# Conditioning units taken in pairs and fours, a column quadrant of TensorE per quarter of the columns, turned by VectorE block transposes

## The reference, cut to what matters

```python
def _modulate(x, g, shift, scale):
    return _rms(x, g) * (1 + scale[:, None, :]) + shift[:, None, :]
...
for l in range(DEPTH):                      # DEPTH = 2
    mod = jax.nn.silu(c) @ p['ada_w'][l] + p['ada_b'][l]      # (1024) @ (1024, 6144)
    sh1, sc1, g1, sh2, sc2, g2 = jnp.split(mod, 6, axis=-1)
    xm = _modulate(x, p['norm_g'][l, 0], sh1, sc1)
...
    x = x + g1[:, None, :] * y
    xm = _modulate(x, p['norm_g'][l, 1], sh2, sc2)
    x = x + g2[:, None, :] * _swiglu(xm, ...)
```

## Time and profile before

| what | value |
|---|---|
| median of 3 runs | 1632.27 us (1632.23 to 1632.67) |
| the profiled execution | 1630.69 us |
| its span in the trace | 1628.4 us |
| PE busy | 1553.3 us, 95% of the span |
| DVE, ACT, POOL busy | 703.1, 375.5, 746.8 us |
| chain that ended last | PE 87%, DVE 5%, ACT 3%, issue 2%, DMA 1% |

### The profile page before, as it was taken

How to read it: one execution, slowest core, us unless ns; L and a number is a source line. 1 busy time by engine, 2 the same in 40 slices (tenths; PEclk the granted TensorE clock), 3 DMA queues, 4 the chain that set the end, 5 groups by cost and what they waited for, 6 DMA issues and landing times.

```text
span 1628.4 us, 30979 instructions
## 1 busy us (share of the span) xinstructions
PE 1553.3 (95%) x11910; PEld 1454.5 (89%) x11910; DVE 703.1 (43%) x1280; ACT 375.5 (23%) x877; POOL 746.8 (46%) x424
## 2 busy tenths in 40 slices
PE   4999999999999999999999996888999999999999
PEld 2898898999999999999988795656899999999998
DVE  4502354443333123346864056787454442144421
ACT  3411555221110011111220122676321110011100
POOL 3244432444445544455544443144355555455553
PEclk9999999999999999999999998899999999999999
DMA  9245323334444333443222153121122222222231
GB/s 362 81 164 176 113 88 100 128 131 145 141 151 148 131 117 132 151 169 121 93 76 73 70 206 107 54 78 31 52 78 77 83 95 81 72 83 77 85 115 65
DMA packets 53906, 183.18 MB, mean 112 GB/s; under 512 B 6232, under 2 KB 8672, under 8 KB 53584
## 3 DMA queue, kind: packets, MB, share of 16 engines
q1 hardware_dynamic: 51136, 174.63, 31.6%
q10 hardware_dynamic: 2704, 7.64, 1.2%
HBM read 171.69 MB, written 10.55 MB: 112 GB/s over the span
## 4 chain that ended last, share of the span: by engine, by line
PE 87%; DVE 5%; ACT 3%; issue 2%; DMA 1%; POOL 0%; ACTq 0%; DVEq 0%; SPq 0%; POOLq 0%
PE psum L542 67%; PE psum L590 7%; PE psum L552 3%; PE psum L930 1%; DVE act_lo L1430 1%; PE psum L973 1%; PE psum L833 1%; PE psum L917 1%; DVE tmp L1419 1%; DMA raw<-in_w_stream 1%; PE psum L563 1%; PE psum L945 1%; PE psum L853 1%; PE psum L730 1%; ACT sc L1289 1%
## 5 line engine op out<-in xcount | busy, mean ns | idle before, releaser
L473 POOL TENSOR_SCALAR w_hi<-raw 128x1024 fp32r<-128x1024 f32 (+1 forms) x184 | 212.1, 1153 | 748.2 <-PE psum L542 628.8
L475 POOL TENSOR_TENSOR w_lo<-raw,w_hi 128x1024 fp32r<-128x1024 f32 (+1 forms) x184 | 485.1, 2636 | 15.3
L542 PE MATMUL psum<-act_hi,w_hi 128*128 128x288 f32 x2144 | 473.3, 302 | 11.3 <-POOL w_lo L475 4.8
L542 PE MATMUL psum<-act_lo,w_hi 128*128 128x288 f32 x2144 | 463.0, 297 | 0.0
L542 PE MATMUL psum<-act_hi,w_lo 128*128 128x288 f32 x2144 | 462.8, 297 | 0.0
L542 PEld LDWEIGHTS psum<-act_hi,w_hi 128*128 128x128 f32 x2144 | 345.8, 190 | 30.7 <-issue 17.5
L542 PEld LDWEIGHTS psum<-act_hi,w_lo 128*128 128x128 f32 x2144 | 348.0, 190 | 0.0
L542 PEld LDWEIGHTS psum<-act_lo,w_hi 128*128 128x128 f32 x2144 | 347.1, 189 | 0.0
L542 PE MATMUL psum<-hid_hi,w_hi 128*128 128x288 f32 x704 | 151.1, 296 | 0.0
L542 PE MATMUL psum<-hid_lo,w_hi 128*128 128x288 f32 x704 | 150.8, 296 | 0.0
L542 PE MATMUL psum<-hid_hi,w_lo 128*128 128x288 f32 x704 | 150.8, 296 | 0.0
(11 more groups left out here) (259 smaller groups left out, 1684.9 us busy)
## 6 DMA issues: line engine op xcount, KB each, us to landing
raw<-in_w_stream SPq DMA_DIRECT2D x153, 512.0 KB, 3.3
ada_ring<-in_ada_w SPq DMA_DIRECT2D x80, 512.0 KB, 3.3
raw<-in_w_down SPq DMA_DIRECT2D x32, 704.0 KB, 4.0
ada_first<-in_ada_w SPq DMA_DIRECT2D x8, 1024.0 KB, 12.5
line_rep<-line SPq DMA_DIRECT2D x8, 352.0 KB, 4.5
line<-line_rep SPq DMA_DIRECT2D x8, 352.0 KB, 5.2
x<-in_x SPq DMA_DIRECT2D x4, 576.0 KB, 5.7
dec<-line SPq DMA_DIRECT2D x8, 288.0 KB, 4.0
```

The lines of the kernel that those rows point to most:

```text
L473: pool.tensor_scalar(hi, src, 1.0, 0.0, ALU.mult, ALU.add).then_inc(hi_split, 1)
L475: pool.tensor_tensor(lo, src, hi.bitcast(F32), ALU.subtract).then_inc(lo_split, 1)
L542: last = mm(psum[:, b + half, 0:n_cols], weights[wp][:, k, :], parts[ap][:, k, half * HT:half * HT + n_cols], start=(k == 0 and n == 0), s ...
```

## The change

- `matvec` now takes two or four units at once. Quadrant j computes the columns 32j to 32j+31 of each of them over all eight k tiles: 32 matmuls, each with 32 stationary columns and 64 (a pair) or 128 (a four) moving columns. The result stands in PSUM as two full rows per quadrant, so that nothing is left to add.
- ACT's row copies and PE's turns are gone. DVE turns the rows by a block transpose of 32x32 (`ve.transpose`) and adds the bias.
- Units 16 to 47 go in 16 pairs, behind every second projected unit; a pair fills both slots of the ring, and its loads wait for the pair before. Units 48 to 95 go in 12 fours, ten of them behind four projected units of the first FFN and two around its first down units; each has a buffer of 2 MB (`ada_quad`) in the place of the unused second activation buffer, whose four loads wait for the four before. None is left among the queries of the attention.
- The loops of PE that held one conditioning unit behind each projected unit are written out or hold four units.
- At the start the table for the line of biases goes first, the squares of the input have three buffers and not one, the first four pairs of conditioning units are computed ahead of the first step, and the others stand between the steps.

```diff
 
-                if n0 >= ADA_START + 2:
-                    sp.wait_ge(ada_mv, i * 2 + (n0 - ADA_START - 1))
+                p = (n0 - ADA_START) // 2
+                if p >= 1:
+                    sp.wait_ge(ada_mv, i + p)
                 sp.dma_start(ada_ring[:, n0 % 2].rearrange("p k c -> p (k c)"), ada_w[i * 2 + n0]).then_inc(ada_in[n0 % 2], 16)
+
+            def load_quad(q, parts):
+
+                if q == 0:
+                    sp.wait_ge(unit_done, U_OUT + 8)
+                else:
+                    sp.wait_ge(quad_mv, q)
+                for j in parts:
+                    sp.dma_start(ada_quad[:, j].rearrange("p k c -> p (k c)"), ada_w[ADA_QUADS + 4 * q + j]).then_inc(quad_in, 16)
 
...
             sp.dma_start(sml[:, :], small).then_inc(params_ready, 16)
-            sp.dma_start(oh_sb[:, :], oh_line).then_inc(line_in, 16)
-            sp.dma_start(tab_sb[:, :], table).then_inc(line_in, 16)
             for g in range(KT):
+                if g == 6:
+                    sp.wait_ge(line_done, 2)
+                    sp.dma_start(line_dram[:, 0, :], line_sb[:, :]).then_inc(line_stored, 16)
                 if g >= 6:
-                    sp.wait_ge(ada_row_mm, g - 5)
+                    sp.wait_ge(first_mv, g - 5)
                 sp.dma_start(ada_first[:, g % 6].rearrange("p u k c -> p u (k c)"),
                              ada_w[g:g + KT + 1:KT].rearrange("u p n -> p u n")).then_inc(ada_first_in[g], 16)
                 if g < 2:
                     load_unit(g)
...
                 load_rows(h)
-            load_pairs(U_O, 19, 30)
+            load_pairs(U_O, 9, 30)
+
+            def load_four(u0, q):
+
+                for j in range(4):
+                    load_unit(u0 + j)
+                    if j >= 1:
+                        load_quad(q, (j - 1,) if j < 3 else (2, 3))
+
+            for n in range((FH - 1) // 2):
+                load_four(U_FFN0 + 2 + 4 * n, n)
             sp.wait_ge(state_stored, 128)
 
...
 
-            def matvec(out, w, done):
-
-                for kk in range(2):
+            def matvec(rows, w, done):
+
+                for k in range(KT):
                     for j in range(4):
-                        last = mm(out(slice(32 * j, 32 * j + 32)), cs_col(2 * j + kk), w(2 * j + kk), start=(kk == 0), stop=(kk == 1))
+                        r = slice(32 * j, 32 * j + 32)
+                        last = mm(by_unit(rows[r]), cs_col(k), w(k)[:, :, r], start=(k == 0), stop=(k == KT - 1))
                 last.then_inc(done, 1)
 
-            def ada_rows(n0, i=0):
-                s = n0 % 2
-                pe.wait_ge(ada_in[s], i * 16 + 16 * ((n0 - ADA_START) // 2 + 1))
-                matvec(lambda r: psum[r, row_bank(n0), 0:P], lambda k: ada_ring[:, s, k, :], ada_mv)
-
-            def ada_turn(n0, i=0):
-
-                pe.wait_ge(row_ready, i * 2 + (n0 - ADA_START + 1))
-                mm(psum[:, 5, bass.ds(i * 4 + 2 * n0, 2)], row_sb[:, n0 % 2, :], ada_sel, start=True, stop=True).then_inc(ada_done, 1)
-
-            def modulate(n0, i=0, first=False):
-                if not first:
-                    ada_turn(n0 - 1, i)
-                ada_rows(n0, i)
+            def modulate(p):
+
+                for half in range(2):
+                    pe.wait_ge(ada_in[half], 16 * (p + 1))
+                matvec(pair_rows(p), lambda k: ada_ring[:, :, k, :], ada_mv)
+
+            def modulate_four(q, i=0):
+
+                pe.wait_ge(quad_in, i * 64 + 64 * (q + 1))
+                pe.wait_ge(quad_free, i + (q + 1))
+                matvec(quad_rows, lambda k: ada_quad[:, :, k, :], quad_mv)
 
             def project_values(u0, a, tails, ada0=None, between=None):
...
-            pe.wait_ge(params_ready, 64)
-            norm_sums(N_IN)
             pe.wait_ge(line_in, 32)
...
@@ -621,35 +641,29 @@
                 for u in range(2):
                     project(u, 0, act[0], ready=(lo_ready[A_IN], 1), k0=k, k1=k + 1 if k < KT - 1 else None)
 
-            pe.wait_ge(sel_ready, 1)
+            def first_pair(g):
+
+                pe.wait_ge(ada_first_in[g], 16)
+                if g >= 4:
+                    pe.wait_ge(mod_first, g - 3)
+                elif g == 2:
+                    pe.wait_ge(ms_read, 1)
+                matvec(first_rows(g), lambda k: ada_first[:, g % 6, :, k, :], first_mv)
+
+            pe.wait_ge(silu_ready, 3)
+            for g in range(4):
+                first_pair(g)
             for g in range(KT):
-                pe.wait_ge(ada_first_in[g], 16)
-                if g >= 2:
-                    pe.wait_ge(ada_row_ready, g - 1)
-                elif g == 1:
-                    pe.wait_ge(ms_read, 1)
-                matvec(lambda r: psum[r, 4 + 3 * (g % 2), 0:2 * P].rearrange("p (u c) -> p u c", u=2),
-                       lambda k: ada_first[:, g % 6, :, k, :], ada_row_mm)
-                if g >= 2:
-                    first_step(g - 2)
-                pe.wait_ge(ada_row_ready, g + 1)
-                if g >= 1:
-                    pe.wait_ge(mod_first, g)
-                for u in range(2):
-                    mm(psum[:, 5, 2 * (g + KT * u):2 * (g + KT * u) + 2], ada_row[:, g % 2, u, :], ada_sel,
-                       start=True, stop=True).then_inc(ada_done, 1)
-            first_step(KT - 2)
-            first_step(KT - 1)
+                first_step(g)
+                if g < 4:
+                    first_pair(g + 4)
             pe.wait_ge(mod_first, KT)
             project(U_Q + 1, 0, act[0], weights=w_q1)
-            modulate(16, first=True)
-
-            def mixer_pair(i):
-                project(U_Q + 2, i, act[0])
-                modulate(17, i)
-                project(U_Q + 3, i, act[0])
-                modulate(18, i)
-            loop(pe, 3, mixer_pair)
+            modulate(0)
+            for p in range(1, 4):
+                project(U_Q + 2 * p, 0, act[0])
+                project(U_Q + 2 * p + 1, 0, act[0])
+                modulate(p)
 
             def columns():
 
...
+                        loop(pe, (FH - 1) // 2, hidden_four)
+                    else:
+                        loop(pe, FH - 1, hidden_pair)
                     d = f + 2 * FH
                     project(d, 0, hid, nk=FH, ready=(hid_ready, hid0 + FH * hf + 1))
-                    if n0 is not None:
-                        if hf == 0:
-                            modulate(n0 + 2 * FH)
-                        else:
-                            ada_turn(n0 + 2 * FH - 1)
                     project(d + 1, 0, hid, nk=FH)
+                    if quads and hf == 0:
+                        modulate_four(5)
 
                     def down_pair(i):
                         project(d + 2, i, hid, nk=FH)
                         project(d + 3, i, hid, nk=FH)
                     loop(pe, KT // 2 - 1, down_pair)
 
-            ffn(U_FFN0, A_FFN0, N_FFN0, 0, ada0=47)
+            ffn(U_FFN0, A_FFN0, N_FFN0, 0, quads=True)
 
...
             project(U_AQ + 1, 0, act[0], shift=1)
             head_sums(8)
-            modulate(92, first=True)
-            for i in range(3):
+
+            def query_pair(i):
                 project(U_AQ + 2, i, act[0], shift=1)
                 head_sums(9, i)
-                if i == 2:
-                    modulate(95)
                 project(U_AQ + 3, i, act[0], shift=1)
-                if i == 2:
-                    ada_turn(95)
                 head_sums(10, i)
-                if i < 2:
-                    modulate(93 + i)
+            loop(pe, 3, query_pair)
             att_scores(0)
             att_scores(1)
...
             grp = ((0, 0, TP), (1, TP, T))
 
+            def first_square(m):
+
+                if m >= 3:
+                    sa.wait_ge(acc_done, m - 2)
+                af(tmp[:, (0, 3, 4)[m % 3], :], x[:, m, :], ACT.Square).then_inc(sq_ready, 1)
+
             def square_tile(n, m0, i=0):
 
-                if 8 * n + m0 > 0:
-                    sa.wait_ge(acc_done, i * 2 + (8 * n + m0))
-                    separate(sa)
+                sa.wait_ge(acc_done, i * 2 + (8 * n + m0))
+                separate(sa)
                 af(tmp[:, 0, :], x[:, i * 2 + m0, :], ACT.Square).then_inc(sq_ready, 1)
 
             def norm_guess(n):
...
-            def ada_out(n0, i=0):
-                s = n0 % 2
-                sa.wait_ge(ada_mv, i * 2 + (n0 - ADA_START + 1))
-                if n0 >= ADA_START + 2:
-                    sa.wait_ge(ada_done, i * 2 + (n0 - 1))
-                af(row_sb[:, s, :], psum[:, row_bank(n0), 0:P], ACT.Copy).then_inc(row_ready, 1)
-
-            def rows_out(g):
-                sa.wait_ge(ada_row_mm, g + 1)
-                if g >= 2:
-                    sa.wait_ge(ada_done, 2 * (g - 1))
-                af(ada_row[:, g % 2], psum[:, 4 + 3 * (g % 2), 0:2 * P].rearrange("p (u c) -> p u c", u=2),
-                   ACT.Copy).then_inc(ada_row_ready, 1)
-
             for m in range(KT):
...
```

(22 more changed lines are left out.)

204 lines of the change are left out of this document (92 added, 112 removed).

## The result

The changed kernel takes 1579.58 us (median of 4 runs, 1577.54 to 1584.19), the kernel before 1632.47 (4 runs, 1632.23 to 1634.39): a ratio of 0.9677, 95% interval 0.9654 to 0.9701, so 3.2% faster. The profiled execution took 1580.67 us, 50.0 less than that of before. The changed kernel, run once more among the experiments, gave 1578.82 (5 runs, 1575.04 to 1582.41).

What follows compares the result with a forecast made beforehand. PE was taken to bound the kernel (87% of the chain), except in the start up to 59.4 us. Start 10.6, pairs 6.4, special pairs 3.0, fours 17.6, waits 0.4 and 1.8 made 39.8 us: 1592 us, range 1585 to 1610.

Steps and rivals of the forecast that it cites:

- Price of a unit, pair and four: PE time per conditioning block: one unit 0.88 us before; a pair 1.26, say 1.30, and a four 2.05 after.
- rival of the queue: PE's instruction queue sets the pace, slower than before, in pairs and fours: 45 us worse, 1677; chance 5%.
- a quadrant's rounds don't shorten: Rival: in pairs, 64-column rounds cost as much as 128, a pair 2.05 us; total 1610; chance 17%.
- The start: Up to 59.4 us: more square buffers, pairs computed ahead, no row or turn; gain 10.6 us (7.5 to 12.5).
- nothing comes back to PE without row and turn: In the start's steps, the loop through ACT and DVE vanishes; last group ends at 48.7 instead of 59.3 us.
- The special pairs: Two pairs where PE waits anyway, at 178.96 and 284.91 us: 1.4 and 1.6, together 3.0 us gained.
- Fours: 12 blocks of four conditioning units, each 2.05 us against 3.52, giving 1.47 apiece: 17.6 us gained.
- the turn's wait: PE's wait for a row at 350.50 us goes: 0.4 us gained.
- the late load: Among the attention's queries, a raw load SP held behind a conditioning load comes sooner: 1.8 us gained.
- Costed at nothing: DVE's transposes and bias adds in FFN slack, ACT's vanished rows and SP's load order in fours: no change counted.
- ACT's rows that vanish: nothing but the waits above: Removing ACT's row copies gains only through the PE waits already listed, nothing further.
- SP's order in the fours: First FFN: third and fourth weight loads wait behind the matvec, yet stay hidden if landing under 10 us; cost nothing.

Runs made afterwards that it cites:

- Experiment 6: Changed kernel, with each pair's second unit computed only in the first k tile, so most rounds have 32 columns and outputs are incomplete: 1573.9 us (one run).
- experiment 5: Changed kernel with two, then three, pairs of conditioning units ahead of the first step instead of four: 1594.94 us and 1579.28 us.
- experiment 1: Changed kernel, with SP's loads for attention head 0 waiting until the last query unit is projected: 1582.74 us.
- Experiment 3: Changed kernel, with DVE's last gains of the first FFN waiting until POOL has split the third down unit: 1583.36 us.
- experiment 2: Changed kernel, with DVE's last gains of the first FFN waiting for the first down unit of its second half: 1578.51 us.
- Experiment 7: Last head's sums behind five k tiles, not two, in the attention's output projection: changed kernel 1573.56 us, repeated 1574.27; kernel before with this edit 1634.08.
- after_again: Changed kernel unedited, run once more on the same chip as the repeat with late sums: 1578.82 us (5 runs).
- dve_locked: Same run as Experiment 3: changed kernel, DVE's last first-FFN gains held until POOL split the third down unit; 1583.36 us.

## Why the prediction was wrong

- **How much was missed.** The forecast's median lies 12 us above the measured one. By the table 49.4 us were gained for 39.8, 9.6 more. The other 2.7 are the step from profile to median: the forecast added 1.6, and the changed kernel's median lies 1.1 below its profile.
- **Price of a unit, pair and four: right.** 0.89 each by the pairing, 1.22 (forecast 1.26, rounded up to 1.30) and 2.08 (2.05). The rounds of 64 columns are 0.056 apart. The rounding up was the error: 14 pairs gave 7.7 us, not 6.4 (0.9 of it stands in the FFN's part of the table). The queue did not hold them: no gap in a pair but those named "issue" at the start. (In the recorded rival of the queue, the 84 and the 0.86 cannot be redone from the figures given: 28 blocks of 32 matmuls make 0.90 us for each ns of d. Nothing else hangs on them.) The rival that a quadrant's rounds don't shorten fell. The rule of the Trainium skill weighed there ("TensorE: Matmul & The Clock Gate", section "The mechanism", weight loads overlap only across row groups) does not set the price here: these quadrants share their rows, and 64 columns cost half of 128. Experiment 6 shows that fewer columns than 64 still cost less.
- **The start: right in size, the size of its parts less so.** 10.4 for 10.6, with parts that missed in both directions. The first step came at 29.02, the late end of 25.5 to 29.5: the three operations that finish rstd took 2.49, 1.47 and 2.80 us on DVE beside POOL's splits, 0.76 each when alone. The steps came nearer together than forecast: 1.6 us for the last four, where 1.85 was reckoned. That nothing comes back to PE without row and turn was wrong as put: with two pairs ahead DVE's gains still tie each step to a pair of PE (experiment 5). I did not see that depth decides; that the kernel's four pairs are deep enough was not foreseen.
- **The special pairs** gave 1.4 and 1.8 (3.0 forecast), though PE's wait near 179 did not fall under 0.5 as forecast: 0.86 is left, now for ACT's vm. **Fours, the turn's wait, the late load**: 14.4 in the first FFN and 3.5 among the queries for 17.6; 2.1 for the late load with its 1.8; about 1 us of turns that stood alone was not counted.
- **The step that failed is "Costed at nothing"**, in "ACT's rows that vanish: nothing but the waits above", and with it the list of waits. I had counted what a turn costs PE and who waits for its row, and not who else waits for the *count* of turns. Two others did: SP, whose loads for head 0 stood behind the last one (4.7 us, of which experiment 1 shows 3.5), and DVE, whose `modulation(48, 92)` at the end of the first FFN stood behind a turn, from where it fell into the lock (4.9 us). Experiment 3 shows the lock and its price; that the turn was what brought DVE into it is read from the trace of before (2.72 for L563), and experiment 2 shows that in the changed kernel a wait for the same unit does not do it. So the turn's part in the 4.9 us is argued, the lock's is shown. Both waits were in the trace of before with their releaser: 5.19 for vc_sb and 2.79 for act_lo. Together they are 9.6 us, as much as the table's whole miss: the 2.6 lost in the attention's output projection cancel the small gains elsewhere.
- **The 2.6 us lost** in the attention's output projection are a matter of the granted clock on both sides. Before, PE came there at the low clock (1135.0 to 1145.3), took 4.0 us longer over the same matmuls and did not wait. The changed kernel came at the full clock, waited 2.67, and lost 2.5 at the low clock behind the wait and 1.6 in a second low stretch, behind the wait of 3.00 for POOL; before has that wait too (3.00 at 1160.37), without a low clock behind it. Experiment 7 shows what the first wait and its clock cost. Which clock an execution has on arrival differs between executions of one kernel: after_again came at the low one (1081.6 to 1091.8), did not wait, and left the place no sooner or later (0.1 us) than the first profile.
- **Costed at nothing and right**: DVE's transposes (0.31 us each beside the hidden tiles), SP's order in the fours: PE never waits for POOL between 342 and 760.

## What to carry to other kernels

When an operation goes, list everybody who waits on its semaphore, on every engine and in the DMA queues, and look in the trace for their waits at that count; its busy time is the smaller part. Work computed ahead needs as many steps of lead as the loop through the other engines has, here three at least: with two the same change at the start loses 15 us. And when an engine waits with independent work standing behind the wait, reorder: here three k tiles moved ahead of one pair of matmuls gave 4.5 us.

## What the runs showed of the hardware

- **DVE and POOL.** act_lo is two DVE instructions, each of which reads two SBUF tiles, 0.75 and 0.28 us long when alone. Where the short one started within POOL's w_lo (which also reads two), it took 3.2 us (2.4 beside the last, shorter ones) and ended 0.08 after it, in the kernel before and in dve_locked. Where the long one started 1.2 to 1.7 us into it, in the changed kernel, it took 2.1 to 2.6 and ended 0.55 after. So DVE is not slowed in proportion: it hardly moves until POOL's instruction is done. DVE, ACT and POOL can stay in such a phase: DVE was 6.1 to 6.6 us late for six units of 8.8 us.
- **The clock behind a wait.** A wait of 2.67 us, within which the clock was still up (mean 0.90 from 1088 to 1091), was followed by a granted clock of 0.50 until 1097.2, in which pairs took 0.68 for 0.43. Without wait and low clock PE was 5.3 us sooner, so this wait cost about twice its length. Not every wait has this effect: behind the wait of 3.00 us for POOL the clock stayed at 1.00 in the kernel before and fell in the changed one (1110.9 to 1114.3).
- **Executions of one kernel differ where PE waits.** Two profiles of the changed kernel, the first and after_again, keep their distance to 0.03 us from 342 to 950; at the wait at 267 it had moved by 1.5, and after_again is 1.8 us sooner at 1040, 2.1 later at 1088, 2.9 sooner at 1100 and 1.9 behind. In these runs a kernel that PE bounds in 90% of its time still has a spread of 7 us.
- **32-column quadrants.** The starts of four quadrants lie 0.007 us apart; a round takes about 0.11 us with 128 columns, 0.056 with 64, and about 0.034 with 32 (experiment 6).
